# Fourteen steps of a two-layer trunk on one core: seven half-width products and eight gate chunks in another order on TensorE

## What is computed

```
def conv_ffn(h, w_up, w_dw, b_dw, w_down):
    up = jnp.einsum("bsd,df->bsf", h, w_up)
    act, gate = up[..., :D_FF], up[..., D_FF:]
    act = causal_dwconv(act, w_dw, b_dw)
    return jnp.einsum("bsf,fd->bsd", jax.nn.silu(act) * gate, w_down)
```

## Time and profile before

| | |
|---|---|
| median of three runs | 929.28 us |
| the profiled execution: its time, its span | 928.98 us, 927.2 us |
| TensorE matmul busy | 916.2 us, 5532 matmuls |
| VectorE busy | 613.3 us |
| ScalarE busy | 430.2 us |
| GpSimd busy | 139.2 us |
| mean granted clock of TensorE | 0.998 |
| from the first matmul of one such step to that of the next | 21.08 us |

### The profile page before, as it was taken

How to read it: one execution, slowest core, us unless ns; L and a number is a source line. 1 busy time by engine, 2 the same in 40 slices (tenths; PEclk the granted TensorE clock), 3 DMA queues, 4 the chain that set the end, 5 groups by cost and what they waited for, 6 DMA issues and landing times.

```text
span 927.2 us, 13912 instructions
## 1 busy us (share of the span) xinstructions
PE 916.2 (99%) x5532; PEld 791.6 (85%) x5532; DVE 613.3 (66%) x819; ACT 430.2 (46%) x645; POOL 139.2 (15%) x110
## 2 busy tenths in 40 slices
PE   8999999999999999999999999999999999999997
PEld 7888898888889999988888898888999999888887
DVE  6999986579986666756343468899676666633333
ACT  7653566456444445563222455563545445422330
POOL 0574834000000000056000020000000002800000
PEclk9999999999999999999999999999999999999999
DMA  7323030322223332212323341222222332222212
GB/s 262 116 91 115 9 110 21 117 91 92 69 87 117 93 136 91 92 63 94 125 68 118 112 136 52 95 105 68 92 92 99 125 123 80 94 89 98 93 63 91
DMA packets 22616, 90.03 MB, mean 97 GB/s; under 512 B 2976, under 2 KB 6304, under 8 KB 19104
## 3 DMA queue, kind: packets, MB, share of 16 engines
q1 hardware_dynamic: 21984, 88.72, 28.2%
q10 hardware_dynamic: 576, 0.52, 0.2%
HBM read 86.09 MB, written 2.10 MB: 95 GB/s over the span
## 4 chain that ended last, share of the span: by engine, by line
PE 97%; POOL 1%; DMA 1%; issue 0%; SPq 0%; ACT 0%; DVE 0%; DVEq 0%
PE bank L1530 18%; PE bank L1531 18%; PE bank L1532 18%; PE bank L1843 6%; PE bank L1844 6%; PE bank L1845 5%; PE bank L1823 5%; PE bank L1822 5%; PE bank L1821 5%; PE bank L1572 2%; PE bank L1590 1%; PE bank L1958 1%; DMA w_raw<-w_pw 1%; PE bank L1596 0%; PE bank L1926 0%; PE bank L1607 0%
## 5 line engine op out<-in xcount | busy, mean ns | idle before, releaser
L1043 DVE TENSOR_TENSOR w_lo<-w_raw,w_hi 128x1408 fp32r<-128x1408 f32 (+2 forms) x53 | 99.2, 1872 | 70.2 <-ACT w_hi L604 69.3
L1531 PE MATMUL bank<-u_lo,w_hi 128*128 128x512 f32 (+1 forms) x374 | 140.8, 377 | 0.0
L604 ACT ACTIVATE w_hi<-w_raw 128x1408 fp32r<-128x1408 f32 (+2 forms) x59 | 93.8, 1590 | 98.5 <-PE bank L1532 97.5
L480 POOL TENSOR_TENSOR u_lo<-u_sum,late_hi 128x512 fp32r<-128x512 f32 x32 | 52.1, 1670 | 488.3 <-ACT late_hi L909 488.3
L1530 PE MATMUL bank<-late_hi,w_hi 128*128 128x512 f32 (+1 forms) x272 | 102.6, 377 | 0.0
L1532 PE MATMUL bank<-late_hi,w_lo 128*128 128x512 f32 (+1 forms) x272 | 102.4, 377 | 0.0
L1530 PE MATMUL bank<-f_hi,w_hi 128*128 128x512 f32 x240 | 94.0, 392 | 0.0
L1532 PE MATMUL bank<-f_hi,w_lo 128*128 128x512 f32 x240 | 93.4, 389 | 0.0
L1531 PE MATMUL bank<-f_lo,w_hi 128*128 128x512 f32 x240 | 93.4, 389 | 0.0
L1843 PE MATMUL bank<-as_is,w_hi 128*128 128x512 f32 x224 | 88.3, 394 | 0.0
L1844 PE MATMUL bank<-as_is,w_hi 128*128 128x512 f32 x224 | 88.2, 394 | 0.0
(11 more groups left out here) (262 smaller groups left out, 2178.3 us busy)
## 6 DMA issues: line engine op xcount, KB each, us to landing
w_raw<-w_up SPq DMA_DIRECT2D x56, 512.0 KB, 4.4
w_raw<-w_down SPq DMA_DIRECT2D x32, 704.0 KB, 4.0
w_raw<-w_up SPq DMA_DIRECT2D x16, 1024.0 KB, 4.9
w_raw<-w_pw SPq DMA_DIRECT2D x11, 1024.0 KB, 5.1
x_res<-x SPq DMA_DIRECT2D x3, 512.0 KB, 7.2
out<-out_sb SPq DMA_DIRECT2D x12, 128.0 KB, 2.1
w_raw<-w_pw SPq DMA_DIRECT2D x4, 256.0 KB, 7.0
gathered<-stage SPq DMA_DIRECT2D x32, 32.0 KB, 2.3
```

Source lines behind the costliest of these rows:

```text
L604: nc.scalar.activation(w_hi[s][:, 0:columns], w_raw[s][:, 0:columns], ACT.Copy).then_inc(w_rounded[s], 1)
L1043: V.tensor_tensor(w_lo[s][:, 0:columns], w_raw[s][:, 0:columns], as_f32(w_hi[s][:, 0:columns]), SUB).then_inc(w_split[s], 1)
L1531: M.matmul(dst, a, lo, start=False, stop=False)
```

## The change

The table `TURNS` is written anew. The products keep their order among themselves and so do the chunks; only how they alternate differs. Before: 1, 5, chunk 0, 6, chunk 1, 3, chunk 2, 7, chunk 3, 2, chunk 4, 4, chunks 5, 6, 7. Now: 1, 5, 6, chunks 0 and 1, 3, 7, chunks 2, 3 and 4, 2, 4, chunks 5, 6, 7. No instruction is added or removed, on any engine.

```diff
-TURNS = ((1, None), (5, None), (None, 0), (6, None), (None, 1), (3, None), (None, 2), (7, None), (None, 3),
-         (2, None), (None, 4), (4, None), (None, 5), (None, 6), (None, 7))
+TURNS = ((1, None), (5, None), (6, None), (None, 0), (None, 1), (3, None), (7, None), (None, 2), (None, 3), (None, 4),
+         (2, None), (4, None), (None, 5), (None, 6), (None, 7))
```

## The result

The changed kernel takes 948.44 us (median of 6 runs, 947.85 to 949.27) against 929.38 for the kernel before on the same chips. The ratio is 1.0195, 95% interval 1.0171 to 1.0220: slower, clear of noise, 1.2 us above the forecast and inside the range. The medians alone would give 1.0205; one of the six executions of the kernel before took 935.05. Executions that took far longer than the others of the same kernel are left out of every ratio here. The profiled execution took 948.98 us with a span of 947.2.

A forecast was written before the change was run, and what follows sets the result against it. TensorE, busy 99% of the span, was taken as the bound. Profiled 928.98 + 15.4 (twelve loop waits) + 2.6 (last steps) = 947.0; with the median 0.3 higher, forecast 947.2 us, range 944.4 to 950.2.

The forecast's parts named there:

- The loop on product 6: TensorE waits at product 6 for the chain from product 2: loop 22.36 us against 21.08, twelve times 1.28, 15.4 us.
- rival A: The forecast itself: the loop closes on product 6 in twelve steps, 947.2 us; chance 0.78.
- the restart: TensorE restarting after the wait at product 6: 0.11 us lost, bounds 0 and 0.34, taken from a 512-column event.
- The last steps: Last step of each layer: product 2 comes 1.32 us later, delaying the down-projection; 2 x 1.32 = 2.6 us.
- Three width changes fewer: TensorE's switches between 256 and 512 columns: 0.06 us gained a step, 0.84 us over 14 steps, inside the loop sum.
- The weight load pulled ahead: At product 6, by the Trainium skill's page: restart near 0, loop 0.11 us less, 1.3 us over twelve steps.
- Rival B: No wait appears at product 6, only the width changes go: 928.4 us, not slower; chance 0.06.
- Rival C: The wait at product 6 comes once a layer and doesn't repeat: 5.2 us, so 934.5; chance 0.05.
- Rival D: A second delay joins: restart at its upper bound, VectorE's ten instructions longer, or the clock falls; 950 us, chance 0.09.

## Why the prediction was right

- **The loop on product 6** (rival A) happened as written: where (the twelve steps), for whom (line 882) and how long. Chain 9.44 forecast and measured; TensorE's part 12.76 forecast and 0.11 for the restart, 12.82 measured with the restart in it (387.74 to 400.56); step 22.36 forecast, 22.40 measured. The groups of chunks take 2.75 and 4.11, as forecast.
- **The term that was mis-sized** is the restart: 0.05 us from the release to the first matmul and 0.11 us after it were taken from the 512-column event. Measured are 0.14 (387.60 to 387.74) and about 0.07 (the second matmul comes 0.20 after the first instead of 0.12, and the product takes 1.50 instead of 1.43). Together 0.21 and not 0.16, over twelve steps some 0.5 us. The sum of the two was near by luck in part: the first was set too low and the second too high.
- **The last steps**, 2 x 1.32: shown alone by the run that put them back, 2.5 us by the traces and 2.6 by the waits. The first matmul of the down-projection comes 6.92 us after product 2 (6.97 forecast).
- **Three width changes fewer**, 0.84 us inside the sum: shown by the first step of each layer, which has no wait and is 21.02 us long (21.12 before), and by the run with the copy ahead, whose steps are all 21.02. The two runs that have this gain alone show 0.7 us. The Trainium skill's page TensorE: Matmul & The Clock Gate, in Back-to-back issue gap, has no such term; the runs show it each time.
- **The weight load pulled ahead**, weighed from the same page of the Trainium skill, in Architectural detail, which speaks of loads ahead of matmuls in flight: it did not come ahead. The load started at 387.71 and the matmul at 387.74, both after the copy's end at 387.60. The matmul before had ended at 386.58, so none was in flight.
- **Rival B** fell: the spare time covers either move but not both, as the two runs with one move each show. **Rival C** fell: the wait came in each of the twelve. **Rival D** did not occur in the changed kernel, whose clock was 1.00 throughout these steps, with the gaps of 1.2 us that the prediction weighed. In the two experiments with longer waits the clock did fall (below), and their expectations had no term for it.
- Not in the sum: that the beginning of the program, ahead of any changed instruction, moves by up to 1.6 us from one execution to another. 948.98 - 947.0 = 2.0 is made of 1.6 from there and 0.4 from the changed part. The sum itself was rounded 0.1 low: 947.0 and 0.3 are 947.3, not 947.2.

## What to carry to other kernels

Before moving a piece of TensorE's order, write down for each wait how long its release lies ahead of it, and follow the chain around the loop: one move spends the spare time at its end, another at its beginning, and here each fitted alone while both together closed the loop in every step. A short instruction behind long ones in another engine's order can be what the whole loop waits for; moving a 0.36 us copy gave back 16 us. And when work is moved earlier, check what its producers' own inputs wait for, since the next wait may sit in an engine that was idle before.

## What the hardware showed

**Near waits of TensorE of 2.5 us and more its clock fell, not each time.** In the changed kernel, with gaps of 1.2 to 1.4 us between its matmuls, the granted clock stays at 1.00 to the last 4 us of the program. In the run with product 2 still later, twelve steps have a gap of 2.5 us; at one of them the clock fell 1.9 us into the gap, and product 6 came at half clock. Timeline of TensorE, then the stretches (columns as in the earlier trace rows):

```profile
321.71 0.55 PE L1821 MATMUL bank<-mixed,ring_hi 128*128 128x256 f32 x1 [2.52 <-ACT sq L882]
322.06 0.42 PE L1822 MATMUL bank<-mixed,ring_hi 128*128 128x256 f32 x1
322.28 0.42 PE L1823 MATMUL bank<-mixed,ring_lo 128*128 128x256 f32 x1
```

```profile
321.00:324.50 3.50, 2.79 (x13) 2.82 (x14) 2.43 (x3) 1.49 (x5) 0.00 (x0) 0.52 0.02 5
436.00:440.50 4.50, 0.72 (x3) 0.30 (x2) 3.34 (x3) 3.69 (x6) 4.50 (x3) 1.00 0.00 0
440.60:444.00 3.40, 3.40 (x10) 2.66 (x9) 3.37 (x3) 0.46 (x1) 3.40 (x3) 0.50 0.65 214
```

Matmuls of 256 columns come 0.21 us apart instead of 0.12 while the clock is 0.50, which is 1.2 GHz; that step is 25.04 us instead of 23.77. After the 3.8 us waits at the down-projection the clock falls in both layers, 0.4 and 1.0 us after the matmuls have begun again. In the run with the copy in between, the matmuls of layer 0's down-projection waited 2.5 us (its weight loads 2.9), and the clock fell 1.5 us after they had begun again:

```profile
422.00:425.00 3.00, 0.63 (x3) 0.19 (x1) 2.69 (x2) 2.54 (x5) 3.00 (x3) 1.00 0.00 0
426.60:430.00 3.40, 3.40 (x9) 2.65 (x8) 3.10 (x4) 1.53 (x2) 3.40 (x3) 0.50 0.51 186
```

So a wait near this length cost more than itself in some executions. The runs of the kernel with the copy in between fit this: 940.30 and 939.34 us had a mean granted clock of 0.996, 937.47 of 0.998 and 936.39 of 0.999; only the first was profiled. That the wait is the cause is read from where the falls stand, and no run tested it. Another cause isn't excluded: the kernel before has no such wait in its trace, and the seven executions of 934.9 to 936.8 us show a mean clock of 0.995 to 0.998 too; none of them was profiled.

**The same split took from 1.62 to 2.75 us by what GpSimd was doing when it started.** Why the weight loads of that down-projection waited 2.9 us and not 1.8 is in VectorE's row, line 1043 of the other kernels, and in GpSimd's splits around it:

```profile
422.31 2.75 DVE L1044 TENSOR_TENSOR w_lo<-w_raw,w_hi 128x1408 fp32r<-128x1408 f32 x1 [1.12 <-ACT w_hi L604]
422.31 1.27 POOL L480 TENSOR_TENSOR u_lo<-u_sum,late_hi 128x512 fp32r<-128x512 f32 x1
423.54 2.66 POOL L480 TENSOR_TENSOR u_lo<-u_sum,late_hi 128x512 fp32r<-128x512 f32 x1
```

And layer 1 of the same execution:

```profile
806.01 1.62 DVE L1044 TENSOR_TENSOR w_lo<-w_raw,w_hi 128x1408 fp32r<-128x1408 f32 x1 [1.09 <-ACT w_hi L604]
806.03 2.75 POOL L480 TENSOR_TENSOR u_lo<-u_sum,late_hi 128x512 fp32r<-128x512 f32 x1
```

In layer 0 GpSimd's instruction had started just ahead of VectorE's split (both round to 422.31): it took 1.27 us, and the split ended 1.48 us after it. In layer 1 the split started 0.02 us ahead of GpSimd's: it took its shortest time, and GpSimd's instruction took 2.75 us in place of some 1.3. The thirteen traces hold 73 splits of this size that started while a GpSimd instruction was running, and every one ends 1.48 to 1.56 us after the end of that instruction (of the second one, in the case shown). It is 1.68 us in the kernel before, where 0.20 us of GpSimd's instruction were left; 2.34 where product 2 and 4 stand ahead of chunk 3 in every step, with 0.85 left; and 2.68 with product 2 still later, with 1.19 left, in both layers. Where GpSimd was idle at its start the split took 1.62 or 1.63 us. So these two instructions ran one after the other, and moving TensorE's order changed which came first. That is an account from the traces; no run moved GpSimd's work to test it.
